# A decoder layer on one Trainium2 core: the norm's sum of squares of three recurrent heads, split in two and computed behind the next head's first levels

## The reference, cut to what matters

```
o = <the head's gated linear recurrence, 512 tokens x 128>
o = o * lax.rsqrt(jnp.mean(o * o, axis=-1, keepdims=True) + EPS)
o = o * out_norm.astype(jnp.float32).reshape(HG_HEADS, HG_VDIM)
o = o.reshape(B, T, HG_WIDTH) * jax.nn.silu(g_out.astype(jnp.float32))
```

## Time and profile before

| what | value |
|---|---|
| time, median of 3 runs | 715.07 us (714.61 to 715.69) |
| the profiled execution | 716.16 us, span from first to last instruction 714.4 us |
| PE busy | 694.5 us, 97% of the span |
| DVE busy | 436.5 us, 61% |
| ACT busy | 293.3 us, 41% |
| mean granted TensorE clock | 0.991 of full speed |

### The profile page before, as it was taken

The page is one execution under the profiler, slowest core; times in us unless marked ns, Lnnn a source line. Parts: engine busy times, 40 slices in busy tenths (PEclk is TensorE's granted clock), DMA queues, the critical chain, the costliest instruction groups (busy, mean ns, idle before and its releaser), DMA issues.

```text
span 714.4 us, 10978 instructions
## 1 busy us (share of the span) xinstructions
PE 694.5 (97%) x3944; PEld 548.5 (77%) x3944; DVE 436.5 (61%) x816; ACT 293.3 (41%) x472; POOL 10.4 (1%) x37
## 2 busy tenths in 40 slices
PE   5899999999999999999999999999999999999997
PEld 3666677777767787888788888888888888888885
DVE  3965988888898999988842343332343246434444
ACT  6436563545535344636844233333243132112223
POOL 4000000000000000000000000000000000000000
PEclk9899999999999999999999999999999999999999
DMA  8963222232224757467124553335633324333103
GB/s 292 353 183 89 60 60 61 70 108 59 60 61 118 227 186 242 170 236 217 49 65 142 147 147 104 84 106 147 176 88 88 111 67 148 88 95 110 60 0 119
DMA packets 96155, 89.10 MB, mean 125 GB/s; under 512 B 3110, under 2 KB 85114, under 8 KB 96124
## 3 DMA queue, kind: packets, MB, share of 16 engines
q1 hardware_dynamic: 96124, 88.70, 41.3%
HBM read 86.59 MB, written 2.10 MB: 124 GB/s over the span
## 4 chain that ended last, share of the span: by engine, by line
PE 64%; DVE 2%; issue 0%; DVEq 0%; ACT 0%
PE ps L1384 36%; PE ps L1405 17%; PE ps L1423 6%; PE ps L1697 1%; PE ps L1677 1%; PE ps L1827 1%; PE ps L1444 1%; PE ps L1831 1%; PE ps L1828 1%; PE ps L1690 0%; DVE w_lo L843 0%; PE ps L1800 0%; DVE act L1176 0%; DVE act L918 0%; DVE res L1181 0%
## 5 line engine op out<-in xcount | busy, mean ns | idle before, releaser
L1384 PE MATMUL ps<-h_hi,w_hi 128*128 128x512 f32 x560 | 226.6, 405 | 0.0
L1384 PE MATMUL ps<-h_hi,w_lo 128*128 128x512 f32 x560 | 219.4, 392 | 0.0
L1384 PE MATMUL ps<-h_lo,w_hi 128*128 128x512 f32 x560 | 218.9, 391 | 0.0
L843 DVE TENSOR_TENSOR w_lo<-w_raw,w_hi 128x1024 fp32r<-128x1024 f32 (+1 forms) x109 | 129.2, 1187 | 96.6 <-ACT w_hi L463 96.2
L463 ACT ACTIVATE w_hi<-w_raw 128x1024 fp32r<-128x1024 f32 (+1 forms) x109 | 111.4, 1028 | 108.6 <-PE ps L1405 85.2
L1384 PEld LDWEIGHTS ps<-h_hi,w_hi 128*128 128x128 f32 x560 | 105.6, 189 | 26.4 <-issue 4.7
L1384 PEld LDWEIGHTS ps<-h_hi,w_lo 128*128 128x128 f32 x560 | 105.5, 188 | 22.7
L1384 PEld LDWEIGHTS ps<-h_lo,w_hi 128*128 128x128 f32 x560 | 105.7, 189 | 20.9 <-issue 0.7
L1405 PE MATMUL ps<-w_hi,h_hi 128*128 128x512 f32 x176 | 69.7, 396 | 0.0
L1405 PE MATMUL ps<-w_hi,h_lo 128*128 128x512 f32 x176 | 68.5, 389 | 0.0
L1405 PE MATMUL ps<-w_lo,h_hi 128*128 128x512 f32 x176 | 68.5, 389 | 0.0
(11 more groups left out here) (258 smaller groups left out, 776.7 us busy)
## 6 DMA issues: line engine op xcount, KB each, us to landing
w_raw<-in_w_ffn_in SPq DMA_DIRECT2D x44, 512.0 KB, 6.2
w_raw<-in_w_in SPq DMA_DIRECT2D x28, 512.0 KB, 4.0
w_raw<-in_w_ffn_out SPq DMA_DIRECT2D x22, 512.0 KB, 3.5
adaw<-in_w_ada SPq DMA_DIRECT2D x12, 512.0 KB, 4.0
act<-in_w_ada SPq DMA_DIRECT2D x12, 512.0 KB, 8.7
adaw<-in_w_ada SPq DMA_DIRECT2D x6, 1024.0 KB, 5.2
act<-in_w_ada SPq DMA_DIRECT2D x6, 1024.0 KB, 5.2
res<-in_x SPq DMA_DIRECT2D x8, 512.0 KB, 5.0
```

The source lines that it names most:

```text
L843: V.tensor_tensor(w_lo[slot][:, 0:n], w_raw[slot][:, 0:n], w_hi[slot][:, 0:n].bitcast(f32), ALU.subtract).then_inc(lo_ok, 1)
L1384: last = mm(ps[bank][0:rows, :], a, b, start=(k == 0 and n == 0), stop=(k == KT - 1 and n == 2))
```

## The change

The product by ones (`oss_mm`) of heads 0, 1 and 2 is taken from the end of their body and put into the next head's, behind levels 0 and 1 and the transposes. It becomes two single-pass products, of the rounded squares and of the rest. ACT makes the rounded squares right behind the squares; DVE makes the rest behind the product that readies level 1. The root moves on ACT from the end of a body to the next body, behind the copy of the transposed values, and so do the table loads. `ones_r` is now made ahead of the heads, and PE waits for it once before head 0. The last head keeps its float32 product, and its root stands where it stood. `head_tail` on DVE is not touched, and `sc` is ACT, `te` PE, `V` and `ve` DVE.

```diff
+            def norm_root(h):
+                nc.scalar.preload_act_table_set("natural_log_exp_and_others")
+                sc.wait_ge(oss_mm, h + 1)
+                sc.activation(o_rstd, ps[4][:, :], ACT.Ln, scale=1.0 / HEAD, bias=eps[:, :]).then_inc(oln_ok, 1)
+                sc.wait_ge(oln_ok, h + 1)
+                sc.activation(o_rstd, o_rstd, ACT.Exp, scale=-0.5).then_inc(ors_ok, 1)
+
-            def hg_body(h, last):
-                nc.scalar.preload_act_table_set("sigmoid_and_others")
+            def hg_body(h, first, last):
                 sc.wait_ge(iv_mm, h + 1)
                 sc.activation(i_tok, ps[6][:, :], ACT.Copy).then_inc(iv_ok, 1)
+                if not first:
+                    norm_root(h - 1)
+                nc.scalar.preload_act_table_set("sigmoid_and_others")
...
                 sc.activation(o_sq, ps[7][:, :], ACT.Square).then_inc(osq_ok, 1)
                 if last:
                     att_raw(0, (2,))
+                    norm_root(h)
                 else:
+                    sc.wait_ge(osq_ok, h + 1)
+                    sc.activation(first_hi[:, 0:SEQ], o_sq, ACT.Copy).then_inc(ohi_ok, 1)
                     hg_g(h + 1)
-                nc.scalar.preload_act_table_set("natural_log_exp_and_others")
-                sc.wait_ge(oss_mm, h + 1)
-                sc.activation(o_rstd, ps[4][:, :], ACT.Ln, scale=1.0 / HEAD, bias=eps[:, :]).then_inc(oln_ok, 1)
-                sc.wait_ge(oln_ok, h + 1)
-                sc.activation(o_rstd, o_rstd, ACT.Exp, scale=-0.5).then_inc(ors_ok, 1)
-                if not last:
                     hg_next_hi(h + 1)
...
             hg_g(0)
             hg_next_hi(0)
 
+            sc.activation(ones_r[:, :], ones[:, :], ACT.Copy).then_inc(ones_ok, 1)
             sc.wait_ge(at_zero, 1)
...
                 V.tensor_tensor(q_f, q_silu, f_w, ALU.mult).then_inc(lvl_ready, 1)
                 if isinstance(h, int) and h == 0:
                     split_lo(G_HG + 4, 0)
+                else:
+                    ve.wait_ge(ohi_ok, h)
+                    V.tensor_tensor(first_lo[:, 0:SEQ], o_sq, first_hi[:, 0:SEQ].bitcast(f32),
+                                    ALU.subtract).then_inc(olo_ok, 1)
...
                 last.then_inc(iv_mm, 1)
+                if not first_head:
+                    te.wait_ge(olo_ok, h)
+                    mm(ps[4][:, :], ones_r[:, :], first_hi[:, 0:SEQ], start=True, stop=False)
+                    mm(ps[4][:, :], ones_r[:, :], first_lo[:, 0:SEQ], start=False, stop=True).then_inc(oss_mm, 1)
                 for st in range(1, LEVELS):
...
                 if last_head:
                     att_project(0, 23, 24)
+                    te.wait_ge(osq_ok, h + 1)
+                    mm(ps[4][:, :], ones[:, :], o_sq, start=True, stop=True).then_inc(oss_mm, 1)
                 else:
                     hg_project(h + 1, 31, 32)
-                te.wait_ge(osq_ok, h + 1)
-                mm(ps[4][:, :], ones[:, :], o_sq, start=True, stop=True).then_inc(oss_mm, 1)
...
+            te.wait_ge(ones_ok, 1)
+            hg_body(0, True, False)
```

More of the change, by code:

```diff
@@ L207, in build @@
         lvl_ready, lvl_mm, lvl_out, tot_ok = sem("lvl_ready"), sem("lvl_mm"), sem("lvl_out"), sem("tot_ok")
-        o_mm, osq_ok, oss_mm, oln_ok, ors_ok, on_ok, hg_out = (sem(n) for n in (
-            "o_mm", "osq_ok", "oss_mm", "oln_ok", "ors_ok", "on_ok", "hg_out"))
+        o_mm, osq_ok, ohi_ok, olo_ok, oss_mm, oln_ok, ors_ok, on_ok, hg_out = (sem(n) for n in (
+            "o_mm", "osq_ok", "ohi_ok", "olo_ok", "oss_mm", "oln_ok", "ors_ok", "on_ok", "hg_out"))
         a_raw, a_swap, a_t, a_rope, v_mm, v_ok = (sem(n) for n in ("a_raw", "a_swap", "a_t", "a_rope", "v_mm", "v_ok"))
@@ L704, in _ @@
             hg_next_hi(0)
+            sc.activation(ones_r[:, :], ones[:, :], ACT.Copy).then_inc(ones_ok, 1)
             sc.wait_ge(at_zero, 1)
-            with sc.Fori(0, HG_HEADS - 1) as h:
-                hg_body(h, False)
-            hg_body(HG_HEADS - 1, True)
+            hg_body(0, True, False)
+            with sc.Fori(1, HG_HEADS - 1) as h:
+                hg_body(h, False, False)
+            hg_body(HG_HEADS - 1, False, True)
             def split_x_hi(k):
@@ L740, in att_body @@
                     if last and t == 2:
-                        sc.activation(ones_r[:, :], ones[:, :], ACT.Copy).then_inc(ones_ok, 1)
                         sc.wait_ge(sum_used, KT)
@@ L1603, in _, with hg_body @@
             te.wait_ge(sc_relu, 24)
-            def hg_body(h, last_head):
+            def hg_body(h, first_head, last_head):
                 def level(st):
@@ L1664, in hg_body @@
                     att_project(0, 23, 24)
+                    te.wait_ge(osq_ok, h + 1)
+                    mm(ps[4][:, :], ones[:, :], o_sq, start=True, stop=True).then_inc(oss_mm, 1)
                 else:
                     hg_project(h + 1, 31, 32)
-                te.wait_ge(osq_ok, h + 1)
-                mm(ps[4][:, :], ones[:, :], o_sq, start=True, stop=True).then_inc(oss_mm, 1)
-            with te.Fori(0, HG_HEADS - 1) as h:
-                hg_body(h, False)
-            hg_body(HG_HEADS - 1, True)
+            te.wait_ge(ones_ok, 1)
+            hg_body(0, True, False)
+            with te.Fori(1, HG_HEADS - 1) as h:
+                hg_body(h, False, False)
+            hg_body(HG_HEADS - 1, False, True)
             def logits(h, t, bank):
```

## The result

The changed kernel takes 720.96 us (median of 6 runs, 719.43 to 721.49) against 715.0 before (6 runs, 714.6 to 715.69): ratio 1.0080, 95% interval 1.007 to 1.009. So it is slower by 0.7 to 0.8%, 4.7 to 6.0 us. The forecast was 719.9, in a range of 718.3 to 722.4, with 0.90 on slower; both medians lie in the range.

What follows compares the result with a forecast made beforehand. PE was taken to bound bodies 0 to 2, and DVE at least partly body 3. The terms 1.95 + 0.75 + 0.75 + 1.36 = 4.81 us took the median from 715.07 to 719.9 us, range 718.3 to 722.4.

Steps and rivals of the forecast that it cites:

- PE's gain at an edge: Between two heads, PE reaches the projections 0.32 us earlier per edge; 0.68 without any wait.
- PE's wait for `first_lo`: Behind each edge, PE waits about 0.36 us before the product of the rest of the squares.
- DVE's work of 0.7 us: At each edge, DVE's new subtraction making the rest of the squares, 0.68 us long.
- The root: Behind more of ACT's queue at a body's start, it reaches DVE 1.3 us late, low end 1.2.
- DVE's wait: Before L1089 in three bodies, DVE idles about 1.8 us until ACT delivers the root.
- The bodies: The late root delays level 3, costing 0.75 us in body 1, 0.75 in body 2 and 1.36 in body 3.
- The start: Before level 0 of head 0, PE waits for ACT's ones_r and starts 1.95 us later than before.
- The sum: Total of the start and the three bodies: 1.95 + 0.75 + 0.75 + 1.36 = 4.81 us longer.
- The clock: Rival: clock falls in PE's new waits, 1.6 us each; 721.5 for one, 723.1 for two; chance 0.28.
- The table load: On ACT ahead of each root, 1.29 us from its start to Ln, with nothing behind the load.
- The Trainium skill's drain: Rival: a drain at each root's table switch adds 1.38 us per root, giving 724; chance 0.02.

Runs made afterwards that it cites:

- e3: Changed kernel with ones_r made ahead of head 0's first gate function and the root first on ACT at a body's start: 713.74 us against 714.29, ratio 0.9995.
- e6: e3 with PE's two single-pass products of the sum placed one projection step later: 713.22 us against 714.94, ratio 0.9971.
- e2: Changed kernel with the root ahead of the weight group and the copy on ACT at a body's start: 715.64 us against 714.29, ratio 1.0020.
- e7: Changed kernel with ones_r made early and DVE's use of the root moved from behind level 1 to behind level 2: 714.67 us against 714.94, ratio 1.0000.
- e5: Kernel before the change, with only ones_r made ahead of the heads and PE's wait for it before head 0: 717.68 us against 714.94, ratio 1.0040.
- e1: Changed kernel with ones_r made on ACT ahead of head 0's first gate function: 718.07 us against 714.29, ratio 1.0051.
- e9: Changed kernel run a second time, unedited, beside the filled kernel: 719.44 us against 714.71 for the kernel before, ratio 1.0066.
- e8: e6 with DVE's use of the root moved behind level 2: 716.49 us against 714.94, ratio 1.0017.
- e4: The filled kernel: changed kernel with PE transposing the identity in both long waits (before head 0, before body 3's level 3): 719.3 us against 714.29, ratio 1.0076.
- e10: The filled kernel of e4 run a second time, beside the changed kernel: 720.17 us against 714.71 for the kernel before, ratio 1.0068.

## Why the prediction was right

**PE's gain at an edge** held in its parts. Without the root's delay the three bodies were 0.32, 0.32 and 0.18 shorter (e3 against before); I had 0.32 for PE, and in body 3 DVE decides. Once PE's wait for `first_lo` is covered (e6), bodies 1 and 2 gain 0.32 and 0.29 more; I had 0.36 for that wait. **DVE's work of 0.7 us** and the loop's written-out first body cost nothing that e3 shows.

**The root.** The chain was to end 1.3 late. DVE's L1089 starts 5.88 behind the start of the squares (135.58 - 129.70), for 4.70 before (132.04 - 127.34): 1.18 late. The overlaps between activations, which I had used for the low end of 1.2, all took place. DVE's wait was 1.65 for 1.8, PE's before level 3 0.99 for 1.07, body 3's 1.87 for 1.9. The bodies cost 0.77, 0.74 and 1.28 for 0.75, 0.75 and 1.36; e2 shows that ACT's order is the cause, and e7 that it costs through DVE's use of the root.

**The start** cost 1.95 for 1.95 in the profile, and e5 shows it alone, e1 takes it away.

**The sum** of these is 4.74 for 4.81. The second median lies there (4.73 over its kernel before), the first 1.2 higher.

How close the number came is in part luck. The forecast was for executions without a fall of the clock in the heads, and both profiles of the changed kernel have one or two. The profiled execution was put at 721.0 and took 721.47, but the ledger up to the last head's sum gives 6.91 more, not 4.81: 4.74 and 2.17 for the falls. The 1.22 ahead of the heads and the 0.39 behind them, neither of which the prediction had, take 1.61 of it away, and 5.30 is left.

**The clock** was a rival with 0.28, priced 1.6 for each fall. The first profile has both falls: 1.59 at the start, as priced, and 0.58 in body 3, where DVE is partly the bound and hides the rest; 0.81 in the second profile. With a start wait and nothing to fill it there are four profiles (changed, e2, e5, e9), and the clock fell in one; with the long wait before level 3 of body 3 there are three (changed, e1, e9), and it fell in two; it also fell behind e8's wait of 2.22. In the four places filled with transposes (e4, e10) it never fell. Four of eight against none of four is not enough to show that the filling did it: if it did nothing, the falls would be spread like this about once in seven (an estimate from these counts). I had put 0.52 on no fall at all and 0.28 on one or more; the chance of at least one was too small by these rows. Two executions of e9 had a mean granted clock of 0.996 and 0.997, about that of e4's profile without a fall in the heads (0.997), and took 718.94 and 719.37, like e4's own at 0.997 (718.58 to 719.3). That is 4.2 and 4.7 over their kernel before, so the loss of the sum above is probably there without a fall; only the profiled executions show where the clock fell. What the falls add to the median is open: the filled kernel's median is 1.7 under the changed one's in the first comparison (719.3 and 720.96, on different occasions) and 0.7 over it in the second. The clock's early falls weigh as much: with the one at 64 us the start step begins at about 97.2, without it at about 95.6 (above).

**The table load** took 1.29 from start to next activation (132.91 to 134.20), as before. The Trainium skill's drain on top of it (ScalarE: Activation LUTs, What ACT_TABLE_LOAD costs) is not in this trace either, and the price of 1.38 per root that followed from it did not come.

## What to carry to other kernels

An operation that is moved to a later place in one queue is late for the next engine by what now stands ahead of it, and what it costs is read in the third engine, at the first step that is behind it in the second one's order. Here about 0.6 us per head was to be saved on PE (0.64 and 0.61 in e6), and 1.2 us of lateness on ACT was handed through DVE to PE. Put the part that others wait for first in its queue and then look whether what it displaced has a cover of its own (e6 against e8). A constant that a stage needs belongs in an idle moment well ahead of it: one copy of 0.3 us behind a 1.05 us instruction held the whole of PE for 1.95.

## What the runs showed of the hardware that I had not expected

A wait of PE of 1.9 us with the clock at 2.4 GHz may or may not be followed by a fall to 1.2 GHz: the wait of 1.88 at the start had both outcomes in two executions of the changed kernel. With transposes of the identity in the place of the wait it stayed at 2.4 GHz in all four places (two in e4, two in e10), which is too few to show that they are the reason. In e5 PE started 0.44 us behind the end of the copy that it waited for, where 0.1 is usual (98.05 to 98.15 in the changed kernel); this stays open.
